# A hybrid decoder step: U gathers 36 rows ahead of their V rows in place of 32, a search head moved, dot products between two output halves, and weight padding left in memory

## What is computed

```python
q = (xb @ w_peer_q).reshape(n, PEER_HEADS, 2, PEER_QDIM // 2)
v1, i1 = lax.top_k(s1, PEER_TOPK)          # s1, s2: 128 keys each
v2, i2 = lax.top_k(s2, PEER_TOPK)
...
experts = e1 * PEER_KEYS + e2
g = jax.nn.softmax(vs, axis=-1).astype(xb.dtype)
act = jax.nn.gelu(jnp.einsum('nd,nhkd->nhk', xb, peer_u[experts]), approximate=False)
return jnp.einsum('nhk,nhkd->nd', g * act, peer_v[experts])
```

## Time and profile before

| | us |
|---|---|
| median of three runs | 3788.27 |
| fastest and slowest of them | 3775.75, 3801.06 |
| the profiled execution, its own time | 3769.41 |
| its span on the core | 3767.6 |

### The profile page before, as it was taken

How to read it: one execution, slowest core, us unless ns; L and a number is a source line. 1 busy time by engine, 2 the same in 40 slices (tenths; PEclk the granted TensorE clock), 3 DMA queues, 4 the chain that set the end, 5 groups by cost and what they waited for, 6 DMA issues and landing times.

```text
span 3767.6 us, 35399 instructions
## 1 busy us (share of the span) xinstructions
PE 2508.2 (67%) x11810; PEld 1305.1 (35%) x11810; DVE 2370.3 (63%) x6243; ACT 410.9 (11%) x951; POOL 2403.3 (64%) x2118
## 2 busy tenths in 40 slices
PE   6746665769666777667566756667666766657666
PEld 5633233434334434332234323333344333313201
DVE  3577566667575775766476755766475655846741
ACT  1102000013011221101000110001000110000000
POOL 0147675567754776657756776657765676678775
PEclk9877767878878788888888887888787788886678
DMA  5589989998999989999999999999999999999998
GB/s 178 216 307 352 393 322 383 396 357 319 394 374 350 357 334 387 389 378 386 375 402 379 408 365 404 376 376 384 388 397 357 393 359 384 385 378 367 337 386 321
DMA packets 376057, 1365.51 MB, mean 362 GB/s; under 512 B 61122, under 2 KB 72578, under 8 KB 348354
## 3 DMA queue, kind: packets, MB, share of 16 engines
q0 software_dynamic: 304128, 1107.43, 76.6%
q1 hardware_dynamic: 71746, 255.81, 17.7%
HBM read 1356.76 MB, written 6.31 MB: 362 GB/s over the span
## 4 chain that ended last, share of the span: by engine, by line
POOL 23%; PE 19%; DMA 16%; issue 15%; DVE 13%; another core or an unknown queue 9%; SPq 3%; ACT 1%; ACTq 0%; DVEq 0%; POOLq 0%
POOL u_ring L662 12%; POOL v_ring L673 11%; DMA v_ring<-down_rows,codesT 7%; PE ps L743 7%; DMA wbuf<-weights 6%; PE ps L717 6%; DVE u_ring L1473 3%; DMA u_ring<-up_rows,codes 3%; DVE arena L1443 2%; SPq L569 1%; PE ps L962 1%; PE ps L909 1%; DVE idx L1443 1%; DVE top_c L1443 1%
## 5 line engine op out<-in xcount | busy, mean ns | idle before, releaser
L662 POOL DMA_INDIRECT u_ring<-up_rows,codes x1056 | 1227.0, 1162 | 657.8 <-issue 314.3
L673 POOL DMA_INDIRECT v_ring<-down_rows,codesT x1056 | 1175.1, 1113 | 694.0 <-issue 319.8
L1473 DVE CUSTOM_DVE_ANT_0 u_ring<-u_ring,xn 128x1024 f32<-128x1024 f32 x1056 | 1255.8, 1219 | 548.2 <-DMA u_ring<-up_rows,codes 502.6
L717 PE MATMUL ps<-v_ring,Z 128*32 128x512 f32 x4096 | 1062.9, 790 | 661.2 <-DMA v_ring<-down_rows,codesT 404.0
L743 PE MATMUL ps<-wbuf,xT 128*128 128x256 f32 (+1 forms) x2016 | 516.9, 420 | 224.3 <-DMA wbuf<-weights 186.7
L717 PEld LDWEIGHTS ps<-v_ring,Z 128*32 128x32 f32 x4096 | 177.6, 127 | 1310.3 <-DMA v_ring<-down_rows,codesT 699.8
L743 PEld LDWEIGHTS ps<-wbuf,xT 128*128 128x128 f32 (+1 forms) x2016 | 402.0, 206 | 360.9 <-DMA wbuf<-weights 137.6
L909 PE MATMUL ps<-xT,wbuf 128*128 128x128 f32 (+1 forms) x2304 | 325.1, 299 | 50.7 <-DMA wbuf<-weights 38.4
L909 PEld LDWEIGHTS ps<-xT,wbuf 128*128 128x128 f32 x2304 | 303.8, 212 | 142.3 <-issue 97.6
L1443 DVE MAX8 vals<-arena 128x8 f32<-128x128 f32 (+1 forms) x288 | 69.2, 281 | 112.1 <-ACT arena L1284 61.7
L865 PE MATMUL ps<-kT,qT 96*128 96x512 f32 (+3 forms) x192 | 89.8, 578 | 31.1 <-DVE nb L1447 20.1
(11 more groups left out here) (294 smaller groups left out, 2162.1 us busy)
## 6 DMA issues: line engine op xcount, KB each, us to landing
wbuf<-weights SPq DMA_DIRECT2D x215, 1024.0 KB
u_ring<-up_rows,codes POOLq DMA_INDIRECT x1056
v_ring<-down_rows,codesT POOLq DMA_INDIRECT x1056
resid<-x_prompt SPq DMA_DIRECT2D x8, 512.0 KB
table<-decay_in SPq DMA_DIRECT2D x8, 512.0 KB
table<-ffn_w SPq DMA_DIRECT2D x8, 512.0 KB
kT<-cache_latent SPq DMA_DIRECT2D x64, 64.0 KB
y_prompt<-arena SPq DMA_DIRECT2D x8, 512.0 KB
```

The source lines that it names most:

```text
L662: pool.indirect_dma_start(out=u_ring[:, i % U_RING, :], out_offset=None, in_=up_rows, in_offset=bass.IndirectOffsetOnAxis(ap=codes[:, t % ...
L673: pool.indirect_dma_start(out=v_ring[:, v % V_RING, :], out_offset=None, in_=down_rows, in_offset=bass.IndirectOffsetOnAxis(ap=codesT[:, t ...
L717: mm = pe.matmul(acc[32 * c:32 * c + 32, half, :], (Zs if t == TILES else Z)[:, at:at + GS], v_ring[:, v % V_RING, half * 512:(half + 1) * ...
L1473: dve.tensor_tensor_reduce(u, u, xn[:, t % 2], 1.0, 0.0, ALU.mult, ALU.add, dots[:, k:k + 1]).then_inc(dot_done, 1)
```

## The change

Four things are changed. POOL issues 36 U gathers ahead, and then V of slot v and U of slot v + 36 in turn. `w_uq` and `w_ukv` are loaded without their padding. On DVE head 7 of the search stands ahead of `latents_turned`, with the dots of one more site. In `out` there is one more site, between the third and the fourth piece on PE and between the two additions on DVE, so `OUT` (and the ends of the tables `FRONTS` and `LAST`) have six numbers in place of five, with the same sum.

```diff
-        OUT = [5, 5, 3, 3, 2]
+        OUT = [4, 4, 4, 2, 2, 2]
...
-        LAST = [9, 9, 5, 5, 4] + [3, 3] * H + [2, 2] + [58]
+        LAST = [9, 9, 5, 3, 3, 3] + [3, 3] * H + [2, 2] + [58]
...
-                sp.dma_start(piece_of(t, w), weights[w]).then_inc(w_in_buf[at % 2], 16)
+                n = {N_IN: 2 * 768, N_IN + 1: 2 * 512}.get(w, DC * PIECE)
+                sp.dma_start(piece_of(t, w)[:, 0:n], weights[w][:, 0:n]).then_inc(w_in_buf[at % 2], 16)
...
-            for k in range(GS):
-                u_rows(0, k)
-            for t in range(TILES):
-                for g in range(GROUPS):
-                    for j in range(GS):
-                        v_rows(t, g, j)
-                        if g + 1 < GROUPS:
-                            u_rows(t, (g + 1) * GS + j)
-                        else:
-                            u_rows(t + 1, j)
-            for j in range(GS):
-                v_rows(TILES, 0, j)
+            AHEAD = GS + 4
+            for i in range(AHEAD):
+                u_rows(*divmod(i, SLOTS))
+            for v in range(TILES * SLOTS + GS):
+                v_rows(v // SLOTS, v % SLOTS // GS, v % GS)
+                if v + AHEAD < TILES * SLOTS + GS:
+                    u_rows(*divmod(v + AHEAD, SLOTS))
...
                 for w in range(N_O):
-                    if w == 2:
+                    if w >= 2:
                         slots()
...
             def out_and_peer(t, n, slots, following):
                 turned_copy(t, 1, n, None)
+                slots()
                 slots()
                 slots()
                 h_squares(t, n)
...
                 do(dve.tensor_tensor, resid[0:n, 0:512], resid[0:n, 0:512], bank(2, n), ALU.add)
+                slots()
                 dve.wait_ge(piece_done, PIECE_AT[t, O_0 + 3] + 1)
...
                 head_before(6)
                 slots()
+                head_before(7)
+                slots()
                 latents_turned(t, n)
-                slots()
-                head_before(7)
                 slots()
```

More of the change, by code:

```diff
@@ L439, in hybrid_decoder_step @@
         ATTEND = [4] * H + [5, 5]
-        OUT = [5, 5, 3, 3, 2]
+        OUT = [4, 4, 4, 2, 2, 2]
         FRONTS = {t: PROJECT + QKV + ATTEND + OUT for t in range(TILES)}
-        FRONTS[1] = [3, 2, 3, 2, 3, 3] + [2] * 6 + [1] * H + [2, 2] + [3, 3, 4, 3, 4, 4, 4, 4, 4, 3, 3, 2, 3] + [3, 2, 2, 2, 2]
-        FRONTS[2] = [3, 2, 3, 2, 3, 3] + [2] * 6 + [1, 2, 1, 1, 2, 1, 1, 1, 1, 1] + [3] + [3, 3, 2] * BATCH + [3, 2, 2, 2] + [3, 2, 2, 2, 2]
-        FRONTS[3] = [3, 2, 3, 2, 3, 3] + [2] * 6 + [1, 2, 1, 2, 1, 2, 1, 1, 2, 1] + [2] + [3, 3, 2] * BATCH + [3, 2, 2, 1] + [3, 2, 2, 2, 2]
-        LAST = [9, 9, 5, 5, 4] + [3, 3] * H + [2, 2] + [58]
+        FRONTS[1] = [3, 2, 3, 2, 3, 3] + [2] * 6 + [1] * H + [2, 2] + [3, 3, 4, 3, 4, 4, 4, 4, 4, 3, 3, 2, 3] + [2, 2, 2, 2, 1, 2]
+        FRONTS[2] = [3, 2, 3, 2, 3, 3] + [2] * 6 + [1, 2, 1, 1, 2, 1, 1, 1, 1, 1] + [3] + [3, 3, 2] * BATCH + [3, 2, 2, 2] + [2, 2, 2, 2, 1, 2]
+        FRONTS[3] = [3, 2, 3, 2, 3, 3] + [2] * 6 + [1, 2, 1, 2, 1, 2, 1, 1, 2, 1] + [2] + [3, 3, 2] * BATCH + [3, 2, 2, 1] + [2, 2, 2, 2, 1, 2]
+        LAST = [9, 9, 5, 3, 3, 3] + [3, 3] * H + [2, 2] + [58]
         PEER = [[2, 2], [2, 2], [2, 1], [2, 2], [2, 2], [1, 2], [2, 2], [1, 2], [2, 2]]
@@ L1673, in attention, with out @@
                               over(sums[:], 2, [P, H, 64]), ALU.mult)
-            def out(t, n):
+            def out(t, n, slots):
                 if t == TILES:
@@ L1742, in out_and_peer @@
                 slots()
-                out(t, n)
+                out(t, n, slots)
                 slots()
```

## The result

The changed kernel takes 3929.73 us, the median of four runs (3910.48 to 3940.09), and the kernel before 3782.01 us in four (3748.30 to 3801.06). The ratio is 1.0393, with a 95% interval of 1.0344 to 1.0442: slower by 148 us, where 26 us less were forecast. The profiled execution takes 3923.13 us.

What follows compares the result with a forecast made beforehand. The 16 DMA engines were taken as the bound. Padding -15, lead -13, first U gather +5, end -3 gave -26 us on 3769.4, scaled to 3762 us; forecast 3745 to 3773 (chance 0.46), eight-in-ten range 3712 to 3800.

Steps and rivals of the forecast that it cites:

- 36 in place of 32: POOL's gather order: up to four more U gathers fill projection stalls, 13 us won of 20.4; bounds 0 and 20.4.
- The V ring runs dry: Rival: where POOL waits for dots or codes, V has four rows less; +47 us, 3835 us, chance 0.07.
- The two need each other: Projection stretch: without head 7's move the U ring would be full; without the 36, POOL blocked with dots done.
- The projection: Stalls in five tiles while PE waits for a weight piece: 20.4 us missing to full DMA share, 13 taken as gain.
- The padding: Loads of `w_uq` and `w_ukv`: 6.55 MB fewer on the hardware queue, 15 us won; bounds 0 and 17.1.
- Head 7: DVE's search head ahead of its wait for `latT`: that wait shrinks; price 0 to 4 us a tile, taken 0.
- The output at nothing: Four dots before each second addition on DVE: the 94.8 us wait falls to about 55, no time won; bounds -3, +5.
- The tile's first U gather: POOL's wait for the next tile's codes: four V gathers less queued ahead, 5 us lost; bounds 0 and 38.
- Start and end: Start costs nothing; the last U gather comes four V gathers sooner, shortening the tail by 0 to 5 us, taken 3.
- a rule of the same page of the Trainium skill: All transfers share the same 16 engines; by it gather order alone wins nothing where they are busy.

Runs made afterwards that it cites:

- all but 36: The changed kernel with a lead of 32 in place of 36, all else as changed: 3749.32 us, ratio 0.9914 to the kernel before.
- the two runs on it: Changed kernel with four V gathers moved ahead of each tile's first U gather: 1.0320; with lead 32 but four V gathers held behind it: 1.0018.

## Why the prediction was wrong, step by step

**The step that failed** is "36 in place of 32". It took a gain of 13 us in five stalls of the projection, and closed with "when U is full the V ring holds about five rows in place of nine". That number was right (8 + 33 - 36 is 5, and 9 with a lead of 32), and the sum gave it no price. It holds at every stop of POOL for dots, and the new lead makes these stops more frequent: 117 for 38. PE, and behind it the search, then waits for V rows that stand in the list behind the stopped U gather. The forecast counted the old stops and asked what the new order does in a stretch it knew, in place of asking where the new order would stop. The step measured a loss of 4.8% (0.9914 to 1.0393), some 180 us, in place of the gain of 13.

**The rival "The V ring runs dry"** names the mechanism that happened, with its place (waits for dots or codes) and both of its signs: PE's V wait above 411.9 (632.7) and the mean share below 0.97 (0.94). Its price of +47 us and its chance of 0.07 were wrong. 45 waits x 5.5 us, a quarter uncovered, rest on the number of waits before; with the 117 + 7 waits after and the same quarter it would have been some 170 us. The quarter was a guess, so that this comes near is no proof. The evidence against it, the share of 1.04 in the earlier trace rows, was read from one wait in which a backlog stood behind POOL. A share of 1.02 is seen after the change as well, in the first stop, and 0.69 in the one after it. The missed link is the loop: in the search part DVE's dots wait for scores that PE makes behind a round of V rows, so a stop for one U gather delays the V rows behind it, and through them the dots for which POOL stands next.

**"The two need each other"** (head 7 and the lead) isn't borne out: the lead is no better alone (1.0553), and head 7 with the padding and the site is best without the lead. **The projection** did get shorter, from 779 us in all but 36 to 737 after, over six tiles, three times the 13 I took; but the search loses 133 us over the same tiles.

**The padding** was right: 15 us of 3769 is 0.9960, measured 0.9963. Beside it, the estimate from the fit in "DMA: Bandwidth & Descriptors" (Anatomy of one DMA) in the Trainium skill would have given 2 us less. The page has that fit from transfers issued by GpSimd, and SP issues these; the interval can't tell the two apart. No loss shows in pieces of 0.75 and 0.5 MB.

**Head 7** at nothing: 1.0003. The bounds held.

**The output at nothing** was wrong in size: -0.6%, 23 us with an interval of 7 to 39, where the bounds were -3 and +5. The step "in two of these waits the DMA share is 1.03 and 1.02, so the dots only take rows earlier" took two waits of nine, and looked only inside them. What a filled wait gives can be had later, when the buffers freed there keep POOL going; which stretch gives it back wasn't traced. The wait itself was forecast to fall to 55 us. It did so where the lead is 32 (38.5 alone, 54.6 in all but 36); in the kernel after it rose to 115.3.

**The tile's first U gather** was taken at 5 us with 38 as the upper bound. By the two runs on it, it is 28 or 40 us (0.7 or 1.0%), near the upper bound. In the wait shown above the backlog had drained (0.69), so the four rows fewer were not covered.

**Start and end**: the last stretch is 49 us longer (663 for 614), not 3 shorter. The sample's search runs there, where the same loop is possible; it wasn't traced. Of the some 154 us between the two profiled executions, 123 are in the search of the six tiles, 49 in this stretch and 20 ahead of the six tiles, and the projection gives 40 back.

Beside the forecast stood a rule of the same page of the Trainium skill (Issuing engines are not separate DMA queues), that all transfers share 16 engines. The prediction drew from it that the order of issue wins nothing where they are busy; the page doesn't speak of the order. The trace agrees in the search before, where the share was 1.00. It doesn't follow that the order can lose nothing: between all but 36 and the kernel after only the order differs, and 1.00 became 0.90.

**What stays open**: why a ninth U buffer helps so little at lead 36 (0.4%, not told from nothing), the jump between six and seven rows in hand, how much of the loss in each part of the tile is the loop and how much V rows that are merely late, and where the output site's 0.6% is won.

## What to carry to other kernels

When one in-order queue feeds two rings, work out for each of its possible stops how much of the other ring is in hand, here U_RING + 33 - lead, and keep it well above the batch that the consumer takes at once; the best lead here left two batches of four and one row. A change of lead is to be priced at the stops that it creates and not at the stops that the old profile shows, and above all where the consumer of the one ring waits, over another engine, for the consumer of the other. A stall on one side that shrinks proves nothing until the other side's wait is read beside it.

## What the hardware showed beyond this

A V gather issued while the 16 DMA engines were full took 18.34 us to land (2390.01 to 2408.35), against 1.37 us of DMA time for one gather by the forecast's division; by that figure, an estimate, as much DMA time as 13 gathers went by. At its best POOL issues the two kinds at 0.94 us each and 0.30 between them, 2.5 us a pair, where the DMA engines need 2.7. So after a stop it wins back only some 0.25 us on the DMA engines with each pair, and nothing at the means of the page (1.20 and 1.12 us, 2.9 a pair with the gaps).
